# RWKV scan: the products whose stationary side comes from k run across to the other half of TensorE's array, the values are stored with their two directions exchanged, and b and k results get banks of their own

## The reference

```python
def _wkv_step(S, inp):
    r_t, w_t, k_t, v_t, a_t, b_t = inp
    sa = jnp.einsum('zbhvk,zbhk->zbhv', S, a_t)
    S = S * w_t[..., None, :] + sa[..., :, None] * b_t[..., None, :] + v_t[..., :, None] * k_t[..., None, :]
    return S, jnp.einsum('zbhvk,zbhk->zbhv', S, r_t)

def wkv_bidir(state0, scan_in):
    state, ys = lax.scan(_wkv_step, state0, scan_in)
    ys = jnp.moveaxis(ys, 0, 2)
    return state, ys[0] + ys[1][:, ::-1]
```

## Time and profile before

| what | value |
|---|---|
| median of 3 runs | 4052.1 us |
| the profiled execution: span of its instructions | 4039.7 us |
| TensorE matmul busy | 3727.0 us (92%) |
| VectorE busy | 2360.8 us (58%) |
| ScalarE, GpSimd busy | 1204.0, 1321.7 us |
| the scan, first pairs of head 1 to first pairs of head 15 | 2848.56 to 3365.65 us |

### The profile page before, as it was taken

The page is one execution under the profiler, slowest core; times in us unless marked ns, Lnnn a source line. Parts: engine busy times, 40 slices in busy tenths (PEclk is TensorE's granted clock), DMA queues, the critical chain, the costliest instruction groups (busy, mean ns, idle before and its releaser), DMA issues. The chain is left out here.

```text
span 4039.7 us, 81581 instructions
## 1 busy us (share of the span) xinstructions
PE 3727.0 (92%) x32706; PEld 2683.2 (66%) x32706; DVE 2360.8 (58%) x3864; ACT 1204.0 (30%) x2668; POOL 1321.7 (33%) x1020
## 2 busy tenths in 40 slices
PE   8888999898999999899999997998999999899887
PEld 6667878657787898777344444874999998733333
DVE  4568882545985445565444445767888776623333
ACT  3352222344222322331111112224455454111112
POOL 4443444434445364573000000431555453000000
PEclk9999999999999999999999999999999999899999
DMA  4114542303554122345999995356333234589997
GB/s 128 56 53 170 184 157 93 104 1 105 178 187 146 66 96 75 99 138 228 404 420 420 420 420 212 134 177 201 88 89 91 78 93 147 199 366 422 421 421 316
DMA packets 231204, 787.80 MB, mean 195 GB/s; under 512 B 56008, under 2 KB 64024, under 8 KB 171136
## 3 DMA queue, kind: packets, MB, share of 16 engines
q1 hardware_dynamic: 225008, 764.12, 50.9%
q0 software_dynamic: 5328, 19.40, 1.2%
q10 hardware_dynamic: 576, 0.09, 0.0%
HBM read 736.15 MB, written 47.38 MB: 194 GB/s over the span
## 5 line engine op out<-in xcount | busy, mean ns | idle before, releaser
L2887 POOL DMA_INDIRECT moe0e_xg<-moe_h,moe_first_rows x20 | 18.9, 947 | 546.3 <-DVE moe_first_rows L3044 540.5
L3011 ACT ACT_TABLE_LOAD x32 | 41.1, 1283 | 519.2 <-PE moe1e_p_u L2957 262.4
L373 POOL TENSOR_TENSOR gmi_w_lo<-gmi_rows_w,gmi_w_hi 128x512 fp32r<-128x512 f32 x64 | 120.2, 1878 | 159.8 <-ACT gmi_w_hi L415 159.8
L3960 PE MATMUL scan_bank<-scan_T,scan_off 64*64 64x64 f32 x3840 | 159.4, 220 | 8.5 <-issue 5.7
L373 POOL TENSOR_TENSOR p_w_lo<-p_rows_w,p_w_hi 128x512 fp32r<-128x512 f32 (+3 forms) x88 | 113.5, 1291 | 159.9 <-ACT p_w_hi L415 159.9
L2887 POOL DMA_INDIRECT moe1e_xg<-moe_h,moe_first_rows x17 | 16.0, 940 | 451.0 <-DVE moe_first_rows L3044 444.4
L1159 POOL TENSOR_TENSOR f0u_w_lo<-f0u_w,f0u_w_hi 128x1024 fp32r<-128x1024 f32 x42 | 115.0, 2757 | 137.6 <-ACT f0u_w_hi L1175 137.6
L1159 POOL TENSOR_TENSOR f1u_w_lo<-f1u_w,f1u_w_hi 128x1024 fp32r<-128x1024 f32 x42 | 114.3, 2742 | 137.5 <-ACT f1u_w_hi L1175 137.5
L1227 DVE SCALAR_TENSOR_TENSOR f0u_ada<-hT,condition,f0u_ada 128x512 f32<-128x512 f32 x168 | 148.2, 949 | 16.4 <-DMA hT<-in_ada_w_dram 15.9
L1227 DVE SCALAR_TENSOR_TENSOR f1u_ada<-hT,condition,f1u_ada 128x512 f32<-128x512 f32 x168 | 140.5, 903 | 20.5 <-DMA hT<-in_ada_w_dram 20.0
L2984 PE MATMUL moe0e_p_y<-moe_ring,moe0e_gatedT 128*64 128x512 f32 x608 | 137.6, 605 | 7.8 <-ACT moe0e_gatedT L3013 7.8
(11 more groups left out here) (903 smaller groups left out, 11529.7 us busy)
## 6 DMA issues: line engine op xcount, KB each, us to landing
moe_ring<-in_moe_w_down_dram SPq DMA_DIRECT2D x140, 1024.0 KB, 18.0
gm_uT<-in_moe_w_gu_dram SPq DMA_DIRECT2D x111, 1024.0 KB, 16.6
moe_ring<-in_moe_w_gu_dram SPq DMA_DIRECT2D x102, 1024.0 KB, 24.7
walk_memory<-in_moe_w_gu_dram SPq DMA_DIRECT2D x60, 1024.0 KB, 24.4
hT<-in_ada_w_dram SPq DMA_DIRECT2D x48, 1024.0 KB, 6.8
f0u_w<-in_ffn_w_gate_up_dram SPq DMA_DIRECT2D x22, 1024.0 KB, 4.8
f1u_w<-in_ffn_w_gate_up_dram SPq DMA_DIRECT2D x22, 1024.0 KB, 4.8
gmi_rows_w<-in_ga_w_in_dram SPq DMA_DIRECT2D x64, 256.0 KB, 2.7
```

The lines of the kernel that those rows point to most:

```text
L373: nc.gpsimd.tensor_tensor(w_lo[t % 2][:, 0:width], w[t % RAW][:, 0:width], w_hi[t % 2][:, 0:width], ALU.subtract).then_inc(w_lo_made, 1)
L2887: pool.indirect_dma_start(xg[:], None, H.h, bass.IndirectOffsetOnAxis(rows[:, 0:1], 0)).then_inc(gathered, 16)
L3011: nc.scalar.activation(sg[:], p_g[:], ACT.Silu).then_inc(silu_ready, 1)
L3960: mm = nc.tensor.matmul(out[r], lhsT[r], rhs[r], start=start, stop=stop, skip_group_check=True)
```

## The change: what it does

Every product whose stationary side is made of k, and every product with v, now goes from lo partitions to hi ones and from hi to lo (`crossed`, and `values_to_rows` for y). For that v is loaded with its directions exchanged (forward on hi), the masks of the k parts are exchanged too, and the bonus reads v accordingly. Five pair sets become three groups of four steps (`pair_group`), in which a b product and a k product alternate; b results and k results have separate banks (`BPAIR_BANK`, `KPAIR_BANK`, `TURN_BANK`), separate semaphores, and VectorE masks them separately: six masks instead of five. The products of v into x and y move to the end of the step before; the decay product moves from `walk_state` to `walk_solve`. Since two products into one bank may not come from different halves at once, four semaphores are added on which TensorE waits for itself (`xv_done`, `dsv_done`, `yv_done`, `yr_done`). GpSimd's first masks and its off-diagonal parts alternate. `walk_finish` gets the same walk.

```diff
-    PAIR_SETS = [(0, 1, 2, 3)] + [(j, j + 1) for j in range(CSTEPS, STEPS, 2)]
+    BPAIR_BANK, KPAIR_BANK = (0, 2, 4), (1, 3, 0)
+    TURN_BANK = (1, 3, 1)
@@ load_v
-                    for z, rows in ((0, lo), (1, hi)):
+                    for z, rows in ((0, hi), (1, lo)):
@@ tensor
+                def crossed(out, lhsT, rhs, start=True, stop=True):
+                    for r, o in ((hi, lo), (lo, hi)):
+                        mm = nc.tensor.matmul(out[o], lhsT[r], rhs[r], start=start, stop=stop, skip_group_check=True)
+                    return mm
+                def values_to_rows(i, lhsT, rhs, start=False):
+                    for r, n in ((hi, i), (lo, lat - 1 - i)):
+                        mm = nc.tensor.matmul(y_psum[side(n), n // 2 * HK:n // 2 * HK + HK], lhsT[r], rhs[r], start=start, stop=False, skip_group_check=True)
+                    return mm
@@ walk_state
-                        mmul(x_psum, pairs[u][:, j, 2, :], vs[u][:, j, :], stop=False)
+                        pe.wait_ge(s["xv_done"], w * (STEPS - 1) + j)
                         pe.wait_ge(s["sm_ready"], w * (STEPS - 1) + j)
                         mmul(x_psum, at(w, j), Sm[:], start=False).then_inc(s["x_ready"], 1)
-                    if 0 < j < STEPS - 1:
-                        mmul(ds_psum, bkT[u][:, j, 1, :], vs[u][:, j, :], stop=False)
-                        mmul(ds_psum, eed[w % 3][:, j, :], Sm[:], start=False, stop=False)
+                    if j < STEPS - 1:
+                        crossed(ds_psum, bkT[u][:, j, 1, :], vs[u][:, j, :], stop=False).then_inc(s["dsv_done"], 1)
@@ walk_share
                     if j < STEPS - 1:
                         mmul(ds_psum, bkT[u][:, j, 0, :], SA[:], start=False).then_inc(s["ds_ready"], 1)
...
+                    if j < STEPS - 1:
+                        values_to_x(w, j + 1).then_inc(s["xv_done"], 1)
+                        if i >= -1:
+                            if i == -1 and w:
+                                pe.wait_ge(s["y_copied"], w)
+                            values_to_rows(i + 1, pairs[u][:, j + 1, 3, :], vs[u][:, j + 1, :], start=i == -1).then_inc(s["yv_done"], 1)
@@ pairs
+                    def pair_group(g):
+                        if g == 1 and h:
+                            pe.wait_ge(s["zr_added"], h * NZ)
+                        if g == 2:
+                            pe.wait_ge(s["bpairs_masked"], h * NG + 1)
+                        kinds = 1 if g == 0 else 2
                         wide = kinds * CH
+                        for q in range(4):
+                            j, o = 4 * g + q, slice(q * wide, (q + 1) * wide)
                             rhs = at_rt[h % 3][:, 0:kinds, j, :]
+                            mm_b = mmul(bank[BPAIR_BANK[g]][:, o], bh[:, j, :], rhs)
+                            mm_k = crossed(bank[KPAIR_BANK[g]][:, o], kh[:, j, :], rhs)
@@ turns
                     def turn(g):
+                        if g == 0:
+                            pe.wait_ge(s["kpairs_masked"], h * NG + 1)
+                            pe.wait_ge(s["bpairs_masked"], h * NG + 2)
+                            pe.wait_ge(s["eed_made"], h + 1)
+                        if g == 1:
+                            pe.wait_ge(s["kpairs_masked"], h * NG + 2)
+                            pe.wait_ge(s["bpairs_masked"], h * NG + 3)
+                        if g == 2:
+                            pe.wait_ge(s["tr_copied"], h * NG + 1)
                         for q in range(min(4, STEPS - 1 - 4 * g)):
+                            j, o = 4 * g + q, slice(q * CH, (q + 1) * CH)
+                            mm_b = mmul(bank[TURN_BANK[g]][:, o], bh[:, j, :], eed[h % 3][:, j, :])
+                            mm_k = crossed(bank[TURN_BANK[g] + 1][:, o], kh[:, j, :], eed[h % 3][:, j, :])
```

More of the change, by code:

```diff
@@ L4294, in to_rows, with crossed, values_to_rows @@
                     return mm
+                def crossed(out, lhsT, rhs, start=True, stop=True):
+                    for r, o in ((hi, lo), (lo, hi)):
+                        mm = nc.tensor.matmul(out[o], lhsT[r], rhs[r], start=start, stop=stop, skip_group_check=True)
+                    return mm
+                def values_to_rows(i, lhsT, rhs, start=False):
+                    for r, n in ((hi, i), (lo, lat - 1 - i)):
+                        mm = nc.tensor.matmul(y_psum[(lo, hi)[n % 2], n // 2 * HK:n // 2 * HK + HK], lhsT[r], rhs[r], start=start, stop=False, skip_group_check=True)
+                    return mm
@@ L4323, in walk_share @@
                     if j < STEPS - 1:
-                        mmul(ds_psum, walk.bkT[:, j, 0, :], walk.SA[:], start=False).then_inc(ds_ready, 1)
+                        values_to_x(j + 1).then_inc(xv_done, 1)
+                        if i >= -1:
+                            values_to_rows(i + 1, walk.pairs[:, j + 1, 3, :], walk.v[:, j + 1, :], start=i == -1).then_inc(yv_done, 1)
                 def turn_o(t, h):
```

211 lines of the change are left out of this document (107 added, 104 removed).

## The result

| | before | after |
|---|---|---|
| median (4 runs each, same chip) | 4049.18 us (4043.2 to 4055.37) | 4089.03 us (4086.42 to 4094.18) |
| ratio | | 1.0104, interval 1.0086 to 1.0123 |
| span of the profiled execution | 4039.7 us | 4092.3 us |
| a head, first mask to first mask, mean of 14 | 36.9 us | 40.9 us |
| granted clock, whole span | 0.970 | 0.959 |

47 us faster was forecast, 40 us slower came. Of the 52.6 us between the two profiled spans, the 14 heads alone make 54.9 (571.95 against 517.09 us in the earlier trace rows).

The account below looks back on a forecast made before the run. TensorE was taken as first bound, VectorE close behind. Gains of 3.3 us a head less 0.3 gave 3.0, times 15.5 heads 46.5, plus 1 in `walk_finish`: 47.5 us less, median 4005, own range 3987 to 4022.

Parts of the forecast that it names:

- The added waits: TensorE's new waits for itself in the walk: taken to cost nothing.
- The upper bound: Most the added waits could cost if late: one link's 0.35 us in each of 12 steps, 4 us a head.
- Such 'issue' stops will weigh a little more: TensorE's stops that wait for nothing the profile shows, with less queued: 0.3 us a head off the gain.
- Crossing costs nothing beside a straight product: TensorE's array: a crossed product beside a straight one adds nothing; the straight one keeps its price, 0.117 us.
- Front 1.1, inverse 2.2 us a head: Gains forecast for the front and for the inverse with the rest of the walk, together 3.3 us a head.
- level 0: First level of the inverse: forecast to fall from 4.77 to 4.0 us, a gain of 0.8.
- The floor of 32.7 us a head: TensorE's need per head before the change, summed from product pitches; forecast to fall to 26.4 us.
- Rival 4: Pause before turn 1 drops TensorE's clock in most heads: 29 us slower, 4081 us; chance 0.10.
- Rival 2: Crossing does not pay in runs; pairs and turns cost as before: no change that can be told, 4050 us; chance 0.08.
- Head 0: Has pairs and turns but no walk; counted as half a head of the 3.0 us gain.

Follow-up runs that it names:

- e6: Kernel before, order and products unchanged, plus 37 waits a head on TensorE at the new places, on a signal that came a head earlier: 4088.7 us.
- e10: Changed kernel, still crossed, with TensorE's 37 waits a head for itself replaced by issuing value products ahead of a product whose signal ScalarE answers: 4051.5 us.
- e2: Changed kernel's crossed front with the walk of before: straight products, old order, no waits of TensorE for itself: 4043.3 us, ratio 1.0000.
- e3: Kernel before with only the walk in the changed order and with TensorE's waits for itself, products straight except y's value products: 4088.5 us.
- e7: Kernel before with the walk's new order for x and state, straight, plus TensorE's signals and 22 waits a head for these two: 4059.8 us.
- e12: Kernel before with the walk's new order for x and state, straight, and 21 fewer wait records a head in the inverse: 4034.3 us.
- e9: Kernel before, order unchanged, with 21 fewer TensorE wait records a head in the inverse: 4037.3 us.

## Why the prediction was wrong

**The failing step** is "The added waits [...] I take nothing, the nearest row being the copy for which TensorE waits anyway". It asked how long the awaited thing takes, and that was right: the waits are fulfilled when they are asked for. It left out that a second wait at a product makes a record of its own in TensorE's stream, and that the wait for ScalarE, beside which the new one was put, becomes that record. 27 to 29 such records a head (60 to 62 for 33) cost 33 to 43 us in all: e6 with nothing but them has as much as the whole loss, e10 without them has four fifths of it back. The upper bound, 4 us a head, was near (3.4 in e6); its mechanism, one link of 0.35 us late in each of 12 steps, was not the one: a link where TensorE stands is late by 0.06 us, at 8 places a head.

**"Such 'issue' stops will weigh a little more [...] I take 0.3 off"**: they went from 1.4 to 5.9 us a head. This term of the sum was mis-sized fifteenfold. Row 3024.23 in the earlier trace rows was one of them, at a multiple of 256 records, and the change did touch such stops: most of them had been hidden by what TensorE had queued.

**Crossing costs nothing beside a straight product**: right for the array, 14 to 15 ns a record in runs of eight products, 16 in the earlier trace rows.

**Front 1.1, inverse 2.2 us a head**: neither came; the inverse got 4.0 longer. With the old walk, the crossed front gives nothing (e2: 1.0000, 0.9987 to 1.0012). The head is 37.2 us for 36.9, while the blocks with a stop rose from 22 to 54 and their time by 2.2 us a head. The freed time went there, as I read it, and into the first falls of the clock (0.98). The inverse's sum also took level 0 down by 0.8 us with GpSimd busy 4.77 of its 4.77 us in the earlier trace rows, and gave no reason.

**The floor of 32.7 us a head** was built from pitches and missed what stands between products: no straight kernel with all of its work came below 36.5 us a head, with the fewest waits and full clock. TensorE's busy 35.4 (496 / 14), which the text set aside, lay nearer.

**Rival 4** named the clock, and the clock did fall where it said, next to a stop ahead of turn 1. It is not what the loss rests on: e3 and e6 lose 43 us at 0.99. Its figure per stretch (0.75 of TensorE's time doubled) was too high: 0.25 to 0.37 us for a microsecond. In the changed kernel itself that is still 1.5 to 2.3 us a head (6.2 us at the lower level). By an estimate from e6 (3.4 for the records) and this, crossing gave back 1.0 to 1.8 us a head there, since a head got only 3.9 longer. **Rival 2**, crossing does not pay in runs, was right in its outcome for the front, not in its reason.

**Head 0**, which has no walk and so none of the new waits: the first mask of head 1 comes 3.7 us sooner (2844.88 for 2848.56), where 1.5 was forecast. 1.1 of it lies ahead of head 0 (first mask of head 0 at 2813.14 for 2814.24). The rest, 31.7 us for 34.3, is not crossing's for sure: with the old, straight front the same head lasts 32.0 us in e7 and e12, and 34.5 in e6.

Open: what holds a head at 35.3 to 36.5 us at full clock when records, or half of the inverse's products, are taken out. The ring of TensorE, ScalarE and VectorE in the inverse is my guess; no run took a link out of it.

## What to carry to other kernels

Count instructions, not only array time. In a stream of small products a second wait at one product makes an instruction of its own, even if it is fulfilled long before, and 27 of them a head cost as much as 29 straight products (3.4 us). Look in the trace which of the two waits has become the record: here it was the one for which there was something to wait. Order can replace such a wait, when a product is issued ahead of one whose signal is waited for anyway (e10). Before work is taken off TensorE, look whether it then stands still at a block of its instructions or drops to the lower clock: four kernels with less work (and zeros in a part of it) were 1 to 4% slower.

## What the hardware showed that was not expected

- TensorE stops for 0.9 to 1.0 us in the mean at a multiple of 256 records, 1.4 us after the packet of its next instructions has landed: 22 of 123 blocks in the kernel before, 81 of 124 after.
- A wait that stands alone at its product rides on its weight load; one more makes a record of 0.05 us in the sequencer. The records that a fulfilled wait brought into the walk cost 0.11 to 0.12 us of the kernel's time each (e6, e7), or 0.13 to 0.14 for each that was held; those of the inverse, hardly ever held, some 0.02 (e9: 7.6 us / (15 x 21)).
- Where TensorE stands at a wait, the weight load starts 42 ns after the signal if the wait rides on it, 104 ns if the wait is a record (before and e6, `x_copied`).
- Halving the products of the inverse in the changed kernel (with zeros from ScalarE's copies) took the mean clock of the scan from 0.92 to 0.60, and the kernel from 4089 to 4195 us.
- Crossed and straight 64x64 products share their time in runs of eight too: one more product for each 0.06 us, where straight ones alone take 0.117.
